# Scores of two heads, in opposite row halves of TensorE, issued together

## The reference

```python
# stick breaking: 16 heads of width 64, keys strictly before the query
z = einsum('bhqd,bhkd->bhqk', qb, k) * HEAD_DIM ** -0.5
log_keep = where(past, -softplus(z), 0.0)
tail = cumsum(log_keep, reverse=True) - log_keep
w = where(past, exp(log_sigmoid(z) + tail), 0.0)
o = einsum('bhqk,bhkd->bhqd', w, v)

# moba: with 256 tokens one block, so a causal softmax over 16 heads of width 64
p = softmax(where(opos <= cpos, einsum('bhqd,bhkd->bhqk', qc, k_own) * scale, NEG))

# two-map attention: 4 heads, two maps of width 64 each
s = einsum('bqhmd,bkhmd->bhmqk', qi, k) * scale
p = softmax(where(mask, s, -inf))
a = p[:, :, 0] - lam * p[:, :, 1]
o = einsum('bhqk,bkhe->bqhe', a, v)
```

## Time and profile before

| | us |
|---|---|
| median of 3 runs | 4304.86 |
| lowest and highest | 4293.77, 4305.95 |
| profiled execution, time | 4303.91 |
| profiled execution, span | 4302.2 |
| TensorE busy in it | 3126.3 (73%) |
| VectorE, ScalarE, GpSimd busy | 2554.4 (59%), 1103.2 (26%), 1263.1 (29%) |
| mean granted clock of TensorE | 0.862 |

### The profile page before, as it was taken

One profiled execution on the slowest core, in us unless ns is written; L12 is line 12 of the kernel. 1 busy time (PEld: TensorE's weight loads), 2 busy tenths in 40 slices (PEclk: granted clock), 3 DMA queues, 4 the chain that ended last, 5 costly groups with the idle time before them and its releaser, 6 DMA issues.

```text
span 4302.2 us, 45142 instructions
## 1 busy us (share of the span) xinstructions
PE 3126.3 (73%) x17054; PEld 2425.1 (56%) x17054; DVE 2554.4 (59%) x4443; ACT 1103.2 (26%) x1509; POOL 1263.1 (29%) x1110
## 2 busy tenths in 40 slices
PE   7999999989998799999999753433337783333334
PEld 6987999869896598997986441111114561111111
DVE  4554555555544555554543587777764458777776
ACT  3333333233331333334332211111101221111110
POOL 0000000000000000000000067777872027777776
PEclk9999999989999999999999786777678787767766
DMA  5523555435453345552452279999997049999998
GB/s 187 197 108 132 177 181 178 150 103 176 165 192 123 110 147 181 179 208 88 153 177 98 96 268 345 347 347 353 343 373 273 0 163 350 342 344 352 358 350 331
DMA packets 415039, 940.88 MB, mean 219 GB/s; under 512 B 27889, under 2 KB 210193, under 8 KB 414865
## 3 DMA queue, kind: packets, MB, share of 16 engines
q0 software_dynamic: 150048, 546.37, 34.7%
q1 hardware_dynamic: 259744, 390.09, 26.8%
q10 hardware_dynamic: 5072, 2.12, 0.2%
HBM read 937.45 MB, written 1.05 MB: 218 GB/s over the span
## 4 chain that ended last, share of the span: by engine, by line
PE 56%; POOL 24%; issue 9%; DVE 5%; DMA 5%; ACT 1%; ACTq 0%; SPq 0%; DVEq 0%; POOLq 0%
POOL wide_ring L2074 23%; PE bank L624 13%; PE bank L625 13%; PE bank L626 13%; DMA wide_ring<-in_peer_v,pk_idx 4%; PE bank L689 4%; PE bank L668 4%; PE bank L674 1%; PE bank L1001 1%; DVE xn L1432 1%; DVE x_lo L1448 1%; PE bank L704 1%; PE bank L837 0%; DVE resid L1469 0%; ACTq L1027 0%
## 5 line engine op out<-in xcount | busy, mean ns | idle before, releaser
L1001 PE MATMUL bank<-wide_ring,xT 128*128 128x512 f32 x960 | 548.6, 707 | 934.1 <-DMA wide_ring<-in_peer_v,pk_idx 933.9
L624 PE MATMUL bank<-x_hi,wide_hi 128*128 128x256 f32 x3328 | 958.2, 288 | 20.4 <-DVE x_lo L1448 20.0
L625 PE MATMUL bank<-x_lo,wide_hi 128*128 128x256 f32 x3328 | 954.6, 287 | 0.0
L626 PE MATMUL bank<-x_hi,wide_lo 128*128 128x256 f32 x3328 | 954.0, 287 | 0.0
L1001 PEld LDWEIGHTS bank<-wide_ring,xT 128*128 128x128 f32 x960 | 193.5, 221 | 1286.5 <-issue 1278.0
L1321 DVE TENSOR_TENSOR wide_lo<-wide_ring,wide_hi 128x2048 fp32r<-128x2048 f32 x228 | 522.0, 2289 | 493.0 <-ACT wide_hi L1094 493.0
L2057 POOL TENSOR_TENSOR small<-small,minus_half 128x1 f32<-128x1 f32 (+2 forms) x41 | 27.6, 673 | 2622.4 <-DVE small L1455 2276.9
L2074 POOL DMA_INDIRECT wide_ring<-in_peer_u,pk_idx x512 | 625.4, 1221 | 252.3 <-issue 135.3
L624 PEld LDWEIGHTS bank<-x_hi,wide_hi 128*128 128x128 f32 x3328 | 652.7, 196 | 28.9 <-DVE x_lo L1448 24.2
L625 PEld LDWEIGHTS bank<-x_lo,wide_hi 128*128 128x128 f32 x3328 | 652.7, 196 | 2.6
L626 PEld LDWEIGHTS bank<-x_hi,wide_lo 128*128 128x128 f32 x3328 | 651.9, 196 | 0.0
(11 more groups left out here) (271 smaller groups left out, 3798.1 us busy)
## 6 DMA issues: line engine op xcount, KB each, us to landing
wide_ring<-in_ffn_w_gate_up SPq DMA_DIRECT2D x176, 1024.0 KB, 9.5
deep_ring<-in_ffn_w_down SPq DMA_DIRECT2D x88, 1024.0 KB, 5.0
wide_ring<-in_sb_w_qkv SPq DMA_DIRECT2D x12, 2048.0 KB, 12.4
wide_ring<-in_w_in SPq DMA_DIRECT2D x12, 2048.0 KB, 10.1
wide_ring<-in_peer_w_q SPq DMA_DIRECT2D x8, 2048.0 KB, 12.4
wide_ring<-in_moba_w_qkv SPq DMA_DIRECT2D x6, 2048.0 KB, 12.2
deep_ring<-in_sb_w_o SPq DMA_DIRECT2D x8, 1024.0 KB, 8.3
deep_ring<-in_w_out SPq DMA_DIRECT2D x8, 1024.0 KB, 7.6
```

The source lines that it names most:

```text
L624: mm(o, w[0], x[0], start=start, stop=False, skip_group_check=True)
L625: mm(o, w[0], x[1], start=False, stop=False, skip_group_check=True)
L626: return mm(o, w[1], x[0], start=False, stop=stop, skip_group_check=True)
L1001: ins = mm(acc[t][h][:, :], pk_diag[:, s % 2, k], row_at(ph, n)[:, h * 512:(h + 1) * 512], start=first, stop=last, skip_group_check=True)
```

## The change

`scores(h)` is called for even h only and issues the scores of heads h and h + 1, first part and second part in turn. It waits for `masked` of head h - 1, so that both banks are free. The moba loop and the two-map loop get a function of their own that does the same. The latent loop keeps its one. The semaphore `scores` is raised once for each head, as before. Nothing changes on the other engines.

```diff
                 def scores(h):
-                    pe.wait_ge(S["masked"], seen(at.get("masked", 0) + h - 1))
-                    p0, c = HD * (h % 2), h // 2
-                    q, k = sb_qT[p0:p0 + HD, c], sb_kT[p0:p0 + HD, c]
-                    mm(work[h % 2][:, 0:TOK], k[:, 0:P], q, start=True, stop=True)
-                    mm(work[h % 2][:, TOK:TRI], k[:, P:TOK], q[:, P:TOK], start=True,
-                       stop=True).then_inc(S["scores"], 1)
+                    pe.wait_ge(S["masked"], seen(at.get("masked", 0) + h))
+                    q, k = ([x[p0:p0 + HD, h // 2] for p0 in (0, HD)] for x in (sb_qT, sb_kT))
+                    for j in range(2):
+                        mm(work[j][:, 0:TOK], k[j][:, 0:P], q[j], start=True, stop=True)
+                    for j in range(2):
+                        mm(work[j][:, TOK:TRI], k[j][:, P:TOK], q[j][:, P:TOK], start=True,
+                           stop=True).then_inc(S["scores"], 1)
...
                 for i in range(HEADS + 4):
-                    if i < HEADS:
+                    if i < HEADS and i % 2 == 0:
                         scores(i)
...
+            def soft_scores_of_two(ph, u, qk):
+
+                pe.wait_ge(S["masked"], seen(ph.at.get("masked", 0) + u))
+                (q0, k0), (q1, k1) = qk(u), qk(u + 1)
+                mm(work[0][:, 0:P], q0[:, 0:P], k0[:, 0:P], start=True, stop=True)
+                mm(work[1][:, 0:P], q1[:, 0:P], k1[:, 0:P], start=True, stop=True)
+                mm(work[0][:, P:TRI], q0[:, P:TOK], k0, start=True, stop=True).then_inc(S["scores"], 1)
+                mm(work[1][:, P:TRI], q1[:, P:TOK], k1, start=True, stop=True).then_inc(S["scores"], 1)
...
-                    if i < HEADS:
+                    if ph.kind == "moba" and i < HEADS and i % 2 == 0:
+                        soft_scores_of_two(ph, i, qk)
+                    if ph.kind == "mla" and i < HEADS:
                         soft_scores(ph, i, *qk(i))
...
-                    if u < 2 * DA_HEADS:
-                        p0, c = 64 * (u % 2), u // 2
-                        soft_scores(ph, u, m2_qkT[p0:p0 + 64, c], m2_qkT[p0:p0 + 64, 4 + c])
+                    if u < 2 * DA_HEADS and u % 2 == 0:
+                        soft_scores_of_two(ph, u, lambda u: (
+                            m2_qkT[64 * (u % 2):64 * (u % 2) + 64, u // 2],
+                            m2_qkT[64 * (u % 2):64 * (u % 2) + 64, 4 + u // 2]))
```

## The result

The changed kernel took 4277.45 us, the median of 8 runs (4253.51 to 4285.52), against 4302.37 us for the kernel before, run beside it: 24.9 us or 0.58% less by these medians. One of the eight runs of the kernel before was slow (4796.70 us); without it their median is 4299.88 and the difference 22.4 us, and the ratio, which leaves it out, is 0.9934, with a 95% interval of 0.9919 to 0.9949: faster. The forecast counted from 4304.86 us, 2.5 us above the median of the kernel before here. The profiled executions are 4303.91 us before (span 4302.2) and 4277.54 us after (span 4275.8): 26.4 us of span to account for.

A forecast was written before the change was run, and what follows sets the result against it. TensorE was taken to bound the steady stick-breaking loop and moba, with half clock in moba and two-map. Gains of 8.8 (stick breaking), 5.0 (moba) and 3.8 (two-map) sum to 17.6 us: 4287.2 against 4304.86, range 4278 to 4301.

The forecast's parts named there:

- the second pair of stick breaking: Start of the stick-breaking loop, half clock: tails of head 1 no longer stand behind score 3, 0.8 us sooner.
- Overlap: Paired scores: two heads in opposite row halves run together, so the second block, 0.84 us at full clock, costs 0.
- The steady ring: Steady stick breaking: score, mask, ScalarE exponential, value product, next score; 4.59 us for two heads against 5.21, 0.6 a pair.
- The new wait: Each pair waits until both old banks are masked; odd mask ready 0.8 us before it is needed, costed at 0.
- half-clock part: Moba: both halves working at once bring full clock soon after 876; two pairs gain 4.4, 4.5 us with output product.
- full-clock part: Moba later on: the wait for ScalarE's move binds already, so 0.15 us a pair, 0.5 in all.
- Two-map: Two-map loops at half clock: waits before masks 5 and 7 go, 1.9 us a loop, 3.8 for two.
- 1 (no clock in moba): Moba stays at half clock; the gain is 14.7 us, time 4290.2; chance 0.20.
- 3 (no overlap): Steady loop: pairs behind full-height matmuls run one after the other, same TensorE work as before; 4304 us, chance 0.09.
- 4 (the clock falls in the steady loop): Stick breaking: TensorE idling lowers the clock, up to 3.5 us more a pair; about 4313 us, chance 0.05.
- 2 (the other engines keep the time): All paired loops: VectorE's fixed order adds 0.3 us to each ring; gain 9.7 us, 4295, chance 0.16.
- 5 (TensorE is the limit): Rings looser than worked out, so TensorE alone bounds the loops; gain 21.6 us, 4283, chance 0.05.

The follow-up runs named there:

- move-first kernel: Against the changed kernel, ScalarE moves head i-2's turned weights ahead of head i's exponentials in moba and latent attention; 4260.66 us, ratio 0.9910.

## Why the prediction was off, step by step

The direction and the mechanism were right; the size was not. The gain of span is 26.4 us, the sum had 17.6. The 8.8 between them are +5.2 in stick breaking, -1.9 in moba, +1.0 in two-map and +4.4 outside the loops. That the time itself left the range by 0.55 us is partly the lower base: counted from 4304.86 us, the low end allowed a gain of 26.9, and the medians differ by 24.9.

**The step that failed** is the second pair of stick breaking, "The second, at half clock, gains: ... 0.8". I took the low clock at the loop's start as given and priced only the tails' earlier start. It measured 2.8 us a loop (66.40 to 63.59 with this pair alone, 59.40 to 62.25 without it), and the clock stayed at 1.00 there. For the second of these loops the same price was copied, so the miss counts twice: 2 x 2.0 = 4.0 of the 5.2. I asked whether the change would bring the clock back in moba, and whether it would fall in the steady loop, but not whether it would still fall where it fell before. How much of the 0.8 is right where the clock does fall is not shown: the one paired loop of the changed kernel with the fall gained 4.4 or 6.2 us, depending on which profile of the kernel before stands beside it.

**Overlap: right.** A pair costs a block of 0.85 us (0.84 taken), against 1.50 in one half.

**The steady ring: 0.70 a pair instead of 0.6.** TensorE's own 4.37 us are met (0.85 + two times the 1.76 of 312.57 to 314.33), and 0.14 idle is added, not the 0.22 of the worked-out 4.59. That is the other 1.2 of the 5.2 (12 pairs by 0.1). The ring through ScalarE exists as described; taking it away gave 0.03 a pair, so another one is nearly as long, by the trace that through the tails' bank, which I had not looked for.

**The new wait: right, 0.** No score waits for the odd mask in the steady loop. The 1.11 us ahead of 304.22 are at the start, where nothing else was ready.

**Moba: 3.1 instead of 5.0.** The half-clock part was right in size, 4.8 against 4.5: from the first mask to the ninth it takes 27.40 us and took 32.18. My reason for the early clock was not, as far as one profile shows: without overlap the clock is low for 10.2 us instead of 20.5 too, and with it for 6.8. That the moment was right, 11.0 us after the first mask, where "soon after 876" is 11, is then in part luck. The 0.5 of the full-clock part did not come; the masks there are as far apart as before, and the move-first kernel shows why. And 1.7 us went between the ninth mask and the end, where the clock fell once more, for 3.4 us, which I had not foreseen; what made it fall is open.

The rule of the Trainium skill ("TensorE: Matmul & The Clock Gate", Part 4: PE-mode transpose) would have kept moba at half clock. It did not: the clock was at 1.00 from 861.8, and the part before the ninth mask gained 4.8 us, where a clock that stays low was priced at 1.6.

**Two-map: 2.1 and 2.7 instead of 1.9.** The waits ahead of masks 5 and 7 are gone, as described. Both heads in one half gave 1.3 of it, so the overlap, too, plays a part. The second loop ran part of its time at full clock in some executions (22.96, 23.25) and not in others (23.51).

**Rivals.** 1 (no clock in moba), 3 (no overlap) and 4 (the clock falls in the steady loop) did not happen. 2 (the other engines keep the time) is true of moba at full clock only, and there it is ScalarE's order and not VectorE's. 5 (TensorE is the limit) is nearly met in the steady loop, 0.14 of 4.51 us short of it.

**Open.** The 4.4 us outside the loops are not explained. In sum they are no more than what two executions of one kernel differ by there: 3982.3 and 3971.7 after, 3986.7 and 3988.3 before. One part of them comes again, though. The stretch between the first stick-breaking loop and moba went from 494.8 to 488.3 us, and its time at half clock from 34.1 to 20.5. In the three profiles of kernels without pairs it is 494.4 to 494.8 us, with 34.1 at half clock, and in all eleven with any pair 487.0 to 491.6 us, with 17 to 27. One of the eleven, 491.4 us, has only the softmax loops paired, and they come later, so pairing is not the direct cause in each; no run isolates why. Also open is why the clock falls at the start of the loop in all kernels with heads 2 and 3 apart and seldom with them paired. The runs show which issue pattern goes with which level, not what the chip weighs.

## What to carry to other kernels

When a change moves TensorE's work around a stretch at half clock, price both levels for that stretch, the present one and the other: here one early pair, which kept the clock up, was worth 2.8 us a loop, as much as four ordinary pairs. Two scores of 64 rows in opposite halves cost one (0.85 us a block, against 0.84 for one head), if they stand next to each other in the queue; the order within the block is free. And once a queue is shortened, look at which engine's order closes the next ring: moving one ScalarE instruction ahead of two others gave another 7.0 us in moba, more than the 3.1 of the pairing, and 5.3 in latent attention, part of both through the clock.

## What the runs showed of the hardware

- Two 64-row scores in opposite halves, issued head by head, overlap as well as in turn (blocks of 0.86 and 0.85 us). The Trainium skill ("TensorE: Matmul & The Clock Gate", Part 3: Packing small matmuls) has matmuls in distinct row groups run concurrently, and the trace agrees: at 898.71 and 898.72 the two halves of a moba pair start 0.01 us apart. In one half the same passes take 1.50 us.
- At the start of the stick-breaking loop TensorE's granted clock stays at 1.00 with TensorE busy 1.87 of 3.40 us (14 passes), where before it was at 0.57 with 2.35 of 3.40 busy (9 passes). Part of the longer busy time is the low clock's own, but the changed kernel has more idle time there and the higher clock. In the 3.40 us ahead of that both were busy 1.85 us at 1.00, with 16 passes after and 12 before.
- The same program had the clock at 1.00 there in one execution and fell to 0.50 in another: 2.6 us of a loop of 59.4 hang on the execution. The kernel before had the same with 1.8 us (66.40 and 68.19, clock low for 6.8 and 10.2).
